# Router of a mixture-of-experts layer: which operand of the matmul is held in TensorE, the weights or the tokens

## The chip, the cores and the metric

One core of a Trainium2 chip runs the whole program: TensorE (matmul), VectorE, ScalarE, GpSimd, and SyncE, which issues most transfers. The metric is the device time of the kernel in microseconds; lower is better.

## The reference, cut to what matters

A two-layer decoder trunk over 512 prompt tokens and 8 sample tokens, with 1024 channels. Each layer has token mixers and then a feed-forward part: dense in layer 0, top-2 of 8 experts in layer 1.

```python
def moe_swiglu(h, w_router, b_router, w1, w3, w2):
    logits = h.astype(jnp.float32) @ w_router.astype(jnp.float32) + b_router.astype(jnp.float32)
    top_v, top_i = lax.top_k(logits, TOP_K)
    gates = jax.nn.softmax(top_v, axis=-1)
    comb = jnp.sum(jax.nn.one_hot(top_i, N_EXPERTS, dtype=jnp.float32) * gates[..., None], axis=-2)
    ...
    for e in range(N_EXPERTS):
        y = y + comb[..., e:e + 1] * swiglu(h, w1[e], w3[e], w2[e])
    return y
```

`h` has 520 rows of 1024 numbers, `w_router` is 1024 x 8, so the logits are 520 x 8.

## The kernel before, in words

Activations are held transposed: `hT` has the channels on the partitions, in 8 tiles `k` of 128 channels, and the 520 tokens along the free dimension (512 prompt tokens, then 8 sample tokens). The order of the work is written out by hand: each engine has its own program, in order, and semaphores tie them together. A matmul has a stationary operand, which is loaded into TensorE first, and a moving one, which streams past it; the output has the columns of the stationary operand on the partitions.

In the router (lines 943 to 950) the stationary operand is a tile of the router weights, `wrt[:, k, :]`, 128 x 8, and the moving one half of the tokens, 260 columns. The logits so come out with the 8 experts on the partitions, in two banks of `PP[0]`. The normalised and modulated `hT` for it is made just ahead: VectorE scales (line 1441), ScalarE adds the shift tile by tile (line 1197, semaphore `h`), and GpSimd does the 8 sample columns (lines 612 to 614, semaphore `hs`).

ScalarE adds the bias as it evicts the logits to `lgT` (line 1299; the bias is on 8 partitions, `brt[NE, 1]`). TensorE transposes `lgT` in five pieces (line 954), so that tokens are on the partitions, and VectorE copies the result from `PP[1]` to `lg` (lines 1627 and 1628). On `lg` VectorE finds the two largest logits of each token, their indices and a mask (to line 1643). Meanwhile TensorE transposes `hT` back to rows, 128 tokens at a time (`h_rows`, line 962), three tiles ahead of the mask and two behind it, in `PP[2]` and `PP[3]`; ScalarE copies them out (line 1303). Two matmuls on the mask (lines 969 and 970) count how many tokens stand ahead of each in its expert's list; from that VectorE works out each token's place (line 1662).

With the places, GpSimd scatters the rows to a table in DRAM sorted by expert (line 695, ten indirect transfers), SyncE gathers the first expert's rows (line 486), TensorE turns them (line 985), and the experts follow one after the other (lines 1014 and 1026). The code of an expert exists once for each width of its moving operand (144, 160, 176, 208, 256), and a branch on the token count chooses (line 1046).

The two loads of router weights and bias are issued by ScalarE at the very start (lines 1125 and 1126).

Of the kernel before, what the change touches and what calls it, by code (L numbers as in the profile page):

```python
# [9 lines left out]
ALU = mybir.AluOpType  # L10
ACT = mybir.ActivationFunctionType
AX = mybir.AxisListType

P = 128
D = 1024
KD = D // P
SEQ = 512
NS = 8
T = SEQ + NS
HT = T // 2  # L20
# [6 lines left out]
NE = 8  # L27
# [10 lines left out]
NT = (T + P - 1) // P  # L38
# [51 lines left out]
def trunk_program(nc, A, O):  # L90
    ctx = ExitStack()
    with ctx:
        def sb(name, shape, dt=F32):
            return ctx.enter_context(nc.sbuf_tensor(name, shape, dt))
# [19 lines left out]
        def sem(name):  # L114
            return ctx.enter_context(nc.semaphore(name))
# [4 lines left out]
        hT = sb_two("hT", [P, KD, T])  # L120
# [7 lines left out]
        ident = sb("ident", [P, P])  # L128
        ones = sb("ones", [P, P])
        eps = sb("eps", [P, 1])  # L130
        wrt = sb("wrt", [P, KD, NE])
        brt = sb("brt", [NE, 1])
        win = sb("win", [P, 2])
        winv = sb("winv", [P, 2])
        cinv = sb("cinv", [P, 2, POOL])
# [32 lines left out]
        stat2 = sb("stat2", [P, T])  # L168

        lg = sb("lg", [P, NT, NE])  # L170
# [4 lines left out]
        mask = sb("mask", [P, NT, NE])  # L175
# [8 lines left out]
        gate = sb("gate", [P, 2, NT])  # L184
# [33 lines left out]
        hflat = hT[:, :, :].rearrange("p k n -> p (k n)")  # L218
        gate_p, gate_s, gf, diag = (cut(hflat, i * D, D) for i in range(4))
        outs = work  # L220
        lgT = stat2[0:NE]

        def pair_raw(e, f):
            c, s0 = f // 3, (PER_E * e + 2 * (f // 3)) % EXPERT_RING
# [4 lines left out]
        PP = [ctx.enter_context(nc.psum_tensor(f"PP{q}", [P, 2, 512], F32)) for q in range(4)]  # L229
# [13 lines left out]
        def two(ap):  # L243

            return ap.rearrange("p (h n) -> p h n", h=2)
# [14 lines left out]
        wr_in = sem("wr_in")  # L260
# [30 lines left out]
        def norm_step(tag, k, n):  # L291
# [1 line left out]

        ff_done, ff_act, ff_free = sem("ff_done"), sem("ff_act"), sem("ff_free")
        fy_done, fy_free = sem("fy_done"), sem("fy_free")
        R = {k: sem(f"moe_{k}") for k in ["lg", "lg_ev", "lg_tr", "mask", "pre", "route", "gate",
                                          "zero", "h_tr", "h_row", "in_tr", "hn_odd", "hn_even", 
                                          "f_done", "f_act", "f_free", "y_done", "y_free", "yt_tr", "yt_ev",
                                          "y_out", "y_all", "count", "exp_d", "diag", "g_mm", "g_ev", "x_tr", "x_ev",
# [415 lines left out]
        def _(pe):  # L715
# [58 lines left out]
            for j in range(KD):  # L774
                tr = pe.transpose(PP[3][:, 0, j * NQ:(j + 1) * NQ], crow[0:NQ, j * P:(j + 1) * P], ident[0:NQ, 0:NQ])
# [7 lines left out]
            for l in range(DEPTH):  # L783
                with pe.Fori(0, NA) as i:
                    for j in range(ADA_RING):
                        n = 24 * l + ADA_RING * i + j
                        pe.wait_ge(ada_lo, n + 1)
                        pe.wait_ge(ada_row, n + 1)
                        for k in range(KD):
                            for lower, w in enumerate((ahi[:, j % 3], ada_slot(j))):  # L790
                                mm = pe.matmul(PP[0][0:2 * NQ, j % 2, 0:256], r_(cs[:, k, :]), r_(w[:, k, :]),  # L791
                                               start=(k == 0 and not lower), stop=(k == KD - 1 and bool(lower)))
                        mm.then_inc(ada_mm, 1)
                        if j % 3 == 2:
                            pe.wait_ge(ada_row, n + 3)
                            for m in range(2):
                                tr = pe.transpose(PP[1][:, 0, m * P:(m + 1) * P], modrow[:, m * P:(m + 1) * P], ident[:])
                            tr.then_inc(ada_tr, 1)
                if l == 0:
# [3 lines left out]
                    for v in range(DEPTH):  # L803
                        tr = pe.transpose(PP[3][:, 0, v * NROWS:(v + 1) * NROWS], rows[0:NROWS, v, :], ident[0:NROWS, 0:NROWS])
                    tr.then_inc(pro_tr, 1)
                    pe.wait_ge(x_in, 16 * NT)
                    for j in range(KD):
                        if j >= 2:
                            pe.wait_ge(*((pro_dve, 3 + j // 2) if j % 2 == 0 else (pro_act, j // 2)))
                        for t in range(4):  # L810
                            tr = pe.transpose(PP[2][:, j % 2, t * P:(t + 1) * P], xin[:, t, j * P:(j + 1) * P], ident[:])
                        tr.then_inc(pro_tr, 1)
                    for j in range(KD):
                        tr = pe.transpose(PP[3][:, 1, j * NS:(j + 1) * NS], xin[0:NS, 4, j * P:(j + 1) * P], ident[0:NS, 0:NS])
# [6 lines left out]
            for l in range(DEPTH):  # L821
# [7 lines left out]
                for h in range(4):  # L829
                    tr = pe.transpose(PP[3][:, 0, h * P:(h + 1) * P], ws_raw[:, h, :], ident[:])  # L830
                tr.then_inc(s["ws_tr"], 1)
                for ct in range(2):
# [5 lines left out]
                    tr = pe.transpose(PP[0][:, 0, 120 * ct:120 * ct + 120], stD[0:120, c], ident[0:120, 0:120])  # L838
# [28 lines left out]
                for n in range(4):  # L867
                    for ct in range(2):
                        tr = pe.transpose(PP[3][:, n // 2, (n % 2) * W + ct * P:(n % 2) * W + ct * P + P],
                                          proj[:, HOME[B_V] + ct, n * P:(n + 1) * P], ident[:])  # L870
# [5 lines left out]
                for n in range(4):  # L876
                    for ct in range(2):
                        mm = pe.matmul(PP[n // 2][:, n % 2, ct * 256:ct * 256 + 256], vtok[:, n, ct * P:(ct + 1) * P],
                                       wsT[:, 2 * ct:2 * ct + 2, :].rearrange("p h t -> p (h t)"), start=True, stop=True)
# [17 lines left out]
                for n, (a, m) in enumerate(zip(src, TAIL)):  # L897
                    for ct in range(2):
                        tr = pe.transpose(tail_bank(n)[0:m, ct * P:(ct + 1) * P], a[:, ct, :], ident[:])
# [18 lines left out]
                if l == 0:  # L918

                    for h in range(2):
                        if h:
                            pe.wait_ge(fy_free, KD)
                        for f in range(FH):
                            if f >= 2:
                                pe.wait_ge(ff_free, FH * h + f - 1)
                            if h == f == 0:
                                mm = two_products(0, U_FF(0, 0, 0), hT, hlo, range(KD), h_tile(1))
                            else:
                                for w in range(2):  # L930
                                    mm = product(2 * (f % 2) + w, U_FF(h, f, w), hT, hlo, range(KD))
# [12 lines left out]
            pe.wait_ge(*norm_step(3, "hs", 1))  # L944
            for k in range(KD):
                pe.wait_ge(*norm_step(3, "h", k + 1))
                for h in range(2):
                    gemm_r = pe.matmul(PP[0][0:NE, h, 0:HT], wrt[:, k, :], hT[:, k, HT * h:HT * h + HT],
                                       start=(k == 0), stop=(k == KD - 1))
            gemm_r.then_inc(R["lg"], 1)  # L950
            pe.wait_ge(R["lg_ev"], 1)
            for t in range(NT):
                n = min(P, T - P * t)
                tr = pe.transpose(PP[1][0:n, 0, t * NE:(t + 1) * NE], lgT[0:NE, P * t:P * t + n], ident[0:NE, 0:NE])
            tr.then_inc(R["lg_tr"], 1)

            def h_rows(t):
                n = min(P, T - P * t)
# [102 lines left out]
            with pe.If(counts[NE] > NW):  # L1061
                with pe.Fori(0, NE) as e:
                    for w in range(WINDOWS):
                        x = e * WINDOWS + (NE + w)
                        for t in range(2):
                            pe.wait_ge(Rin[t], reg(pe, 16 * x + 16))
                            for j in range(KD):
                                tr = pe.transpose(PP[t][:, j // 4, (j % 4) * P:(j % 4) * P + P], stage[:, t, j * P:(j + 1) * P], ident[:])
                            tr.then_inc(R["in_tr"], 1)
                        pe.wait_ge(R["hn_even"], reg(pe, 4 * x + (4 - 2 * NE)))  # L1070
                        for f in range(ET):
# [4 lines left out]
                            for v in range(2):  # L1076
                                for k in range(KD):
                                    mm = pe.matmul(PP[v][:, f % 2, 0:NW], raw[:, v, k, :], hn[:, k, :], start=(k == 0), stop=(k == KD - 1))
                            mm.then_inc(R["f_done"], 1)
                        pe.wait_ge(R["f_free"], reg(pe, ET * x + ET))  # L1080
                        for q in range(KD):
# [3 lines left out]
                            for k in range(ET):  # L1085
                                mm = pe.matmul(PP[2][:, q % 2, 0:NW], expert_slot(j, ET, 256)[:, k, P * (q % 2):P * (q % 2) + P],
                                               Gn[:, k, :], start=(k == 0), stop=(k == ET - 1))
                            mm.then_inc(R["y_done"], 1)
                        pe.wait_ge(R["y_free"], reg(pe, KD * x + KD))
                        for j in range(KD):  # L1090
                            if j % 4 == 0:
                                pe.wait_ge(R["yt_ev"], reg(pe, 4 * x + j // 2))
                            for t in range(2):
                                tr = pe.transpose(PP[3][:, t, (j % 4) * P:(j % 4) * P + P], yn[:, j, P * t:P * t + P], ident[:])
# [6 lines left out]
            for j in range(KD):  # L1101
                mm = pe.matmul(PP[0][:, j // 4, (j % 4) * P:(j % 4) * P + P], ones[:], diag[:, j * P:(j + 1) * P],
                               start=True, stop=True)
            mm.then_inc(R["g_mm"], 1)
            for j in range(KD):
                tr = pe.transpose(PP[1][0:NS, j // 4, (j % 4) * P:(j % 4) * P + P], mod[:, 1, 8 * GATE2 + j, 1:NQ], ident[:])
# [3 lines left out]
            for t in range(NT):  # L1110
                n = min(P, T - P * t)
# [10 lines left out]
        def _(act):  # L1122
            act.wait_ge(c_in, 32)
            act.activation(crow[0:NQ], crow[0:NQ], ACT.Silu).then_inc(silu_c, 1)
            act.dma_start(wrt[:], A["w_router"][0].rearrange("(k p) e -> p k e", p=P)).then_inc(wr_in, 16)
            act.dma_start(brt[:], A["b_router"][0].rearrange("(e a) -> e a", a=1)).then_inc(wr_in, 16)

            act.wait_ge(const_ready, 1)
            def root(q, dst, n, done):
# [73 lines left out]
            for l in range(DEPTH):  # L1203
# [70 lines left out]
                if l == 0:  # L1274
                    act.wait_ge(*step(l, "tail_out", 16 * 8))
                    for h in range(2):
# [3 lines left out]
                        for f in range(FH):  # L1280
                            n = FH * h + f
# [12 lines left out]
                                upper(U_FY(h, q) + UNIT_SLOTS)  # L1294

            act.wait_ge(R["lg"], 1)
            act.wait_ge(wr_in, 32)
            act.activation(two(lgT), PP[0][0:NE, :, 0:HT], ACT.Identity, bias=brt[:]).then_inc(R["lg_ev"], 1)
            for t in range(NT):  # L1300
                n = min(P, T - P * t)
                act.wait_ge(R["h_tr"], t + 1)
# [15 lines left out]
            for e in range(NE):  # L1318
                for f in range(ET):
                    n = ET * e + f  # L1320
# [48 lines left out]
        def _(dve):  # L1369
# [8 lines left out]
            def link(ins):  # L1378
                dve.wait_ge(dchain, done(ins))
# [243 lines left out]

            link(dve.memset(lg[:], 0.0))
            dve.wait_ge(R["lg_tr"], 1)
            dve.tensor_copy(lg[:, 0:4, :], PP[1][:, 0, 0:4 * NE].rearrange("p (t e) -> p t e", t=4))
            link(dve.tensor_copy(lg[0:NS, 4, :], PP[1][0:NS, 0, 4 * NE:5 * NE]))
            for t in range(NT):
                last = dve.max(vmax[:, t, :], lg[:, t, :])  # L1630
            link(last)
# [140 lines left out]
```

## Time and profile before

| | us |
|---|---|
| median of 3 runs | 1733.9 (1732.95 to 1734.55) |
| profiled execution | 1732.69 |
| its span | 1730.9 |
| TensorE matmul busy | 1488.1 (86%) |
| VectorE busy | 600.9 (35%) |
| ScalarE busy | 461.0 (27%) |
| GpSimd busy | 398.0 (23%) |

The span is the time from the first to the last instruction of one profiled execution. "PE" is TensorE's matmuls, "PEld" its loads of the stationary operand, which overlap them; "DVE" is VectorE, "ACT" ScalarE, "POOL" GpSimd, "SP" SyncE.
### The profile page before, as it was taken

How to read it: one execution, taken by the hardware profiler on the slowest of the kernel's cores; microseconds unless marked ns; L12 is line 12 of the kernel's file. 1: busy time of each engine (PE TensorE's matmuls, PEld its weight loads, DVE VectorE, ACT ScalarE, POOL GpSimd, SP SyncE). 2: the span in 40 equal slices, each digit the busy share in tenths (PEclk: the TensorE clock that was granted, in tenths of full speed). 3: DMA queues.
4: the chain of work that ended last, by engine and by line, in shares of the span. 5: the costliest groups of instructions: out<-in, count | busy, mean ns of one | idle time of the engine just before them, and what ended most of it. 6: DMA issues, size and time to landing. Idle time of an engine off the chain costs nothing.

```text
span 1730.9 us, 26002 instructions
## 1 busy us (share of the span) xinstructions
PE 1488.1 (86%) x11320; PEld 1425.0 (82%) x11320; DVE 600.9 (35%) x815; ACT 461.0 (27%) x646; POOL 398.0 (23%) x288
## 2 busy tenths in 40 slices
PE   5777794797999999998968784999999986999992
PEld 4555694697999999997957682999999986999992
DVE  6757598734102111014696622011110110010115
ACT  6767421433222122222313312111111110010114
POOL 1101571253344333443450512000000000000005
PEclk9999897899999999998988897999999997999995
DMA  9999231113423323233221027589789792658644
GB/s 319 326 308 348 67 98 32 41 59 118 126 74 100 108 74 98 58 101 98 74 73 49 6 71 271 193 272 334 242 286 318 271 309 76 216 164 300 228 146 169
DMA packets 249973, 286.70 MB, mean 166 GB/s; under 512 B 7469, under 2 KB 241599, under 8 KB 249814
## 3 DMA queue, kind: packets, MB, share of 16 engines
q1 hardware_dynamic: 244886, 272.17, 48.4%
q0 software_dynamic: 3760, 12.09, 1.9%
q8 instruction: 103, 1.69, 0.4%
q10 hardware_dynamic: 1200, 0.56, 0.1%
q14 instruction: 24, 0.20, 0.0%
HBM read 266.45 MB, written 19.07 MB: 165 GB/s over the span
## 4 chain that ended last, share of the span: by engine, by line
PE 71%; DVE 15%; DMA 5%; issue 4%; SPq 2%; ACT 2%; POOL 1%; POOLq 0%; DVEq 0%; ACTq 0%
PE PP L746 29%; PE PP L1014 21%; PE PP L1026 11%; DVE work L1499 7%; DMA mem<-in_w_ada 4%; PE PP L759 2%; PE PP L791 2%; DVE stat L1595 2%; PE PP L720 1%; PE PP L731 1%; PE PP L985 1%; PE PP L996 1%; DVE stat L1428 1%; DVE mem L1441 1%; DVE mem_r L1437 1%
## 5 line engine op out<-in xcount | busy, mean ns | idle before, releaser
L746 PE MATMUL PP<-hT_r,mem_r 128*128 128x260 f32 x2624 | 428.5, 284 | 4.6 <-DVE xT L1453 3.2
L1014 PE MATMUL PP<-big,mem 128*128 128x144 f32 (+2 forms) x2816 | 372.9, 295 | 22.8 <-issue 22.0
L1014 PEld LDWEIGHTS PP<-big,mem 128*128 128x128 f32 x2816 | 370.7, 191 | 23.5 <-issue 22.4
L604 POOL TENSOR_TENSOR mem_r<-mem,mem_r 128x1024 fp32r<-128x1024 f32 (+1 forms) x108 | 279.0, 2598 | 407.7 <-ACT mem_r L1141 407.0
L746 PEld LDWEIGHTS PP<-hT_r,mem_r 128*128 128x128 f32 x2624 | 362.5, 189 | 6.5 <-issue 2.5
L746 PE MATMUL PP<-mem_r 128*128 128x260 f32 x1312 | 263.8, 283 | 0.0
L746 PEld LDWEIGHTS PP<-mem_r 128*128 128x128 f32 x1312 | 201.7, 188 | 0.0
L1026 PE MATMUL PP<-big,mem 128*128 128x144 f32 (+2 forms) x1408 | 193.5, 294 | 0.0
L1026 PEld LDWEIGHTS PP<-big,mem 128*128 128x128 f32 x1408 | 186.6, 190 | 0.0
L1689 DVE TENSOR_TENSOR big<-PP,stat 128x256 f32<-128x256 f32 x88 | 37.4, 425 | 394.4 <-ACT stat L1324 394.4
L702 POOL DMA_INDIRECT mem<-y_by_expert,place x10 | 9.9, 986 | 624.5 <-SPq L534 621.8
L1141 ACT ACTIVATE mem_r<-mem 128x1024 fp32r<-128x1024 f32 (+1 forms) x108 | 115.9, 1099 | 118.5 <-DMA mem<-in_w_dense 70.9
L746 PE MATMUL PP<-big_r,mem_r 128*128 128x260 f32 x1056 | 129.4, 284 | 2.9 <-DVE big L1614 2.9
L746 PEld LDWEIGHTS PP<-big_r,mem_r 128*128 128x128 f32 x1056 | 127.7, 188 | 3.6 <-DVE big L1614 3.3
L1324 ACT ACTIVATE stat<-PP 128x256 f32<-128x256 f32 x88 | 33.8, 384 | 361.5 <-PE PP L1014 361.5
L1499 DVE SCALAR_TENSOR_TENSOR work<-big,vec,work 128x512 f32<-128x512 f32 x120 | 127.1, 1135 | 0.0
L1403 DVE TENSOR_TENSOR mem_r<-mem,mem_r 128x2048 fp32r<-128x2048 f32 x48 | 110.0, 2293 | 46.4 <-ACT mem_r L1157 46.4
L791 PE MATMUL PP<-mem_r,cs_r 128*18 128x256 f32 x768 | 104.0, 296 | 19.2 <-DVE mem_r L1403 18.4
L791 PEld LDWEIGHTS PP<-mem_r,cs_r 128*18 128x18 f32 x768 | 77.3, 103 | 43.2 <-DVE mem_r L1403 22.5
L1157 ACT ACTIVATE mem_r<-mem 128x2048 fp32r<-128x2048 f32 x48 | 91.7, 1911 | 25.1 <-DMA mem<-in_w_ada 25.1
L1614 DVE TENSOR_TENSOR big<-PP,work 128x520 f32<-128x520 f32 x22 | 15.4, 700 | 221.6 <-ACT work L1285 221.6
L759 PE MATMUL PP<-hT_r,mem_r 128*128 128x260 f32 x320 | 58.9, 304 | 28.4 <-POOL mem_r L618 25.9
(236 smaller groups left out, 1100.5 us busy)
## 6 DMA issues: line engine op xcount, KB each, us to landing
mem<-in_w_moe SPq DMA_DIRECT2D x48, 1536.0 KB, 8.8
mem<-in_w_ada SPq DMA_DIRECT2D x48, 1024.0 KB, 11.2
mem<-in_w_moe SPq DMA_DIRECT2D x32, 1408.0 KB, 9.4
mem<-in_w_dense SPq DMA_DIRECT2D x20, 1024.0 KB, 5.5
mem<-in_w_in SPq DMA_DIRECT2D x16, 1024.0 KB, 5.4
mem<-in_w_moe SPq DMA_DIRECT2D x16, 1024.0 KB, 6.8
mem<-in_w_dense SPq DMA_DIRECT2D x16, 704.0 KB, 4.7
mem<-in_w_out SPq DMA_DIRECT2D x8, 1024.0 KB, 5.1
```

Of the source, the lines that this page charges most:

```text
L604: pool.tensor_tensor(r_(raw), raw, read_(hi), ALU.subtract).then_inc(w_lo, 1)
L746: mm = pe.matmul(PP[q][:, h, 0:HT], r_(w[:, k, :]), r_(x[:, k, HT * h:HT * h + HT]), start=(i == 0 and w is wh and x is hi), stop=(i == le ...
L759: mm = pe.matmul(PP[q + c][:, h, 0:HT], r_(w[:, k, :]), r_(x[:, k, HT * h:HT * h + HT]), start=(i == 0 and w is wh and x is hi), stop=(i = ...
L791: mm = pe.matmul(PP[0][0:2 * NQ, j % 2, 0:256], r_(cs[:, k, :]), r_(w[:, k, :]), start=(k == 0 and not lower), stop=(k == KD - 1 and bool( ...
L1014: mm = pe.matmul(PP[w][:, f % 2, 0:n], raw[:, w, k, :], hn[:, k, 0:n], start=(k == 0), stop=(k == KD - 1))
L1026: mm = pe.matmul(PP[2][:, q % 2, 0:n], expert_slot(PER_E * e + 8 + q // 2, ET, 256)[:, k, P * (q % 2):P * (q % 2) + P], Gn[:, k, 0:n], sta ...
L1141: act.activation(r_(hi), raw, ACT.Copy).then_inc(w_hi, 1)
L1157: act.activation(r_(ahi[:, j % 3]), ada_slot(j), ACT.Copy).then_inc(ada_hi, 1)
L1403: dve.tensor_tensor(r_(ada_slot(j)), ada_slot(j), read_(ahi[:, j % 3]), ALU.subtract).then_inc(ada_lo, 1)
L1499: dve.scalar_tensor_tensor(acc, gin[:, ct, k:k + SEQ], tap("conv_c_w", k, ct), acc, ALU.mult, ALU.add).then_inc(s["conv_tap"], 1)
L1595: link(dve.reciprocal(st[:], st[:]))
L1689: dve.tensor_tensor(Gn[:, f, :], PP[1][:, f % 2, 0:NW], hactn[:, f % 2, :], ALU.mult).then_inc(R["f_free"], 1)
```

## The change

The operands of the router's matmuls trade places. For each channel tile `k`, four tiles of 128 tokens of `hT` become stationary, one after the other, and `wrt[:, k, :]` with its 8 columns moves past each. The four accumulate in four banks (`PP[0]` and `PP[1]`). The 8 sample tokens have a pass of their own behind that, with 8 stationary columns. The logits then have tokens on the partitions. ScalarE's eviction, the five transposes and the semaphores `lg_ev` and `lg_tr` go; VectorE reads the logits from PSUM and adds the bias itself, in five additions. The bias is loaded to all 128 partitions.

```diff
-        brt = sb("brt", [NE, 1])
+        brt = sb("brt", [P, NE])
...
-        lgT = stat2[0:NE]
...
             for k in range(KD):
                 pe.wait_ge(*norm_step(3, "h", k + 1))
-                for h in range(2):
-                    gemm_r = pe.matmul(PP[0][0:NE, h, 0:HT], wrt[:, k, :], hT[:, k, HT * h:HT * h + HT],
-                                       start=(k == 0), stop=(k == KD - 1))
-            gemm_r.then_inc(R["lg"], 1)
-            pe.wait_ge(R["lg_ev"], 1)
-            for t in range(NT):
-                n = min(P, T - P * t)
-                tr = pe.transpose(PP[1][0:n, 0, t * NE:(t + 1) * NE], lgT[0:NE, P * t:P * t + n], ident[0:NE, 0:NE])
-            tr.then_inc(R["lg_tr"], 1)
+                for t in range(4):
+                    mm = pe.matmul(PP[t // 2][:, t % 2, 0:NE], hT[:, k, P * t:P * t + P], wrt[:, k, :], start=(k == 0), stop=(k == KD - 1))
+            for k in range(KD):
+                mm = pe.matmul(PP[0][0:NS, 0, NE:2 * NE], hT[:, k, SEQ:T], wrt[:, k, :], start=(k == 0), stop=(k == KD - 1))
+            mm.then_inc(R["lg"], 1)
...
-            act.dma_start(brt[:], A["b_router"][0].rearrange("(e a) -> e a", a=1)).then_inc(wr_in, 16)
+            act.dma_start(brt[:], A["b_router"][0].rearrange("(a e) -> a e", a=1).to_broadcast([P, NE])).then_inc(wr_in, 16)
...
-            act.wait_ge(R["lg"], 1)
-            act.wait_ge(wr_in, 32)
-            act.activation(two(lgT), PP[0][0:NE, :, 0:HT], ACT.Identity, bias=brt[:]).then_inc(R["lg_ev"], 1)
...
             link(dve.memset(lg[:], 0.0))
-            dve.wait_ge(R["lg_tr"], 1)
-            dve.tensor_copy(lg[:, 0:4, :], PP[1][:, 0, 0:4 * NE].rearrange("p (t e) -> p t e", t=4))
-            link(dve.tensor_copy(lg[0:NS, 4, :], PP[1][0:NS, 0, 4 * NE:5 * NE]))
+            dve.wait_ge(wr_in, 32)
+            dve.wait_ge(R["lg"], 1)
+            for t in range(4):
+                dve.tensor_tensor(lg[:, t, :], PP[t // 2][:, t % 2, 0:NE], brt[:], ALU.add)
+            link(dve.tensor_tensor(lg[0:NS, 4, :], PP[0][0:NS, 0, NE:2 * NE], brt[0:NS], ALU.add))
```

## Rows read from the trace of the kernel before

**Rows 1.** The page: busy us (share of the span) x instructions, by engine.
```profile
PE 1488.1 (86%) x11320; PEld 1425.0 (82%) x11320; DVE 600.9 (35%) x815; ACT 461.0 (27%) x646; POOL 398.0 (23%) x288
```

**Rows 2.** Chain in order of time, 1028 to 1082: start us, us, what.
```profile
1037.75 9.78 PE PP L948 x32
...
1047.56 0.69 ACT stat L1299
...
1048.30 0.45 PE PP L954 x5
...
1052.72 0.21 DVE mask L1643
...
1057.65 0.18 DVE place L1662
```

**Rows 3.** Stretches: busy us (x count) by engine, then PEclk, DMA share, GB/s.
```profile
1037.70:1043.00 5.30, 5.25 (x13) 1.67 (x14) 3.87 (x7) 4.57 (x7) 0.00 (x0) 0.50 1.06 372
1043.00:1047.60 4.60, 4.52 (x21) 1.66 (x19) 0.00 (x0) 0.04 (x1) 0.00 (x0) 1.00 1.06 373
```

**Rows 4.** Timeline, router: start us, us, engine line op out<-in xcount [idle before].
```profile
1037.75 9.77 PE L948 MATMUL PP<-hT,wrt 128*8 128x260 f32 x32 [6.09 <-POOL hT L614]
...
1042.04 0.13 PEld L948 LDWEIGHTS PP<-hT,wrt 128*8 128x8 f32 x1 [0.30 <-issue]
...
1043.19 3.82 PEld L948 LDWEIGHTS PP<-hT,wrt 128*8 128x8 f32 x18
```

**Rows 5.** Timeline of the mask matmuls; line 1102: min/median/max ns, starts.
```profile
1052.97 0.30 PEld L969 LDWEIGHTS PP<-mask,tri 128*128 128x128 f32 x2 [1.24 <-DVE mask L1643]
1053.19 0.30 PEld L970 LDWEIGHTS PP<-mask,ones 128*128 128x128 f32 x2
...
L1102 PEld LDWEIGHTS PP<-hT,ones x16: 287/333/333, 1692.3 to 1695.5; 128*128 128x128 f32 x16
```

**Rows 6.** Transposes that move 8 columns: timeline; min/median/max ns, starts.
```profile
92.28 0.66 PE L814 MATMUL PP<-ident,big 8*128 8x8 f32 x8
...
L814 PE MATMUL PP<-ident,big x8: 200/201/223, 92.3 to 92.7; 8*128 8x8 f32 x8
```

**Rows 7.** Timeline of VectorE, the two copies of the logits.
```profile
1048.85 0.19 DVE L1627 COPY lg<-PP 128x32 f32<-128x32 f32 x1 [7.28 <-PE PP L954]
1048.95 0.14 DVE L1628 COPY lg<-PP 8x8 f32<-8x8 f32 x1
```

**Rows 8.** Timeline, TensorE's transposes of the first three row tiles.
```profile
1048.66 1.97 PE L962 MATMUL PP<-ident,hT 128*128 128x128 f32 x16
...
1050.87 1.09 PE L962 MATMUL PP<-ident,hT 128*128 128x128 f32 x8 [0.24 <-ACT work L1303]
```

**Rows 9.** Stretches in the prologue, each with the one that follows it.
```profile
90.75:94.10 3.35, 1.84 (x18) 1.42 (x16) 1.37 (x3) 1.94 (x4) 0.00 (x0) 1.00 0.60 176
94.15:97.50 3.35, 3.35 (x8) 2.67 (x9) 0.00 (x0) 3.35 (x7) 0.00 (x0) 0.50 0.99 337
29.30:32.60 3.30, 1.64 (x13) 1.01 (x12) 3.10 (x2) 2.44 (x3) 0.00 (x0) 1.00 1.10 352
32.70:36.00 3.30, 3.24 (x28) 2.42 (x26) 0.93 (x2) 2.17 (x2) 1.18 (x4) 1.00 1.10 349
```

**Rows 10.** Stretches behind the start of two bursts.
```profile
1442.30:1445.70 3.40, 3.40 (x10) 3.31 (x11) 0.00 (x0) 0.00 (x0) 0.00 (x0) 0.50 0.02 5
1445.85:1449.00 3.15, 3.15 (x20) 3.15 (x19) 0.00 (x0) 0.00 (x0) 0.00 (x0) 1.00 0.00 0
...
1695.00:1698.30 3.30, 3.30 (x18) 2.64 (x17) 1.68 (x2) 1.15 (x1) 2.39 (x4) 0.50 0.88 322
```

**Rows 11.** Chain at a branch between experts; the page's queue of instructions.
```profile
1422.66 19.54 issue
...
q8 instruction: 103, 1.69, 0.4%
```

**Rows 12.** Transfers of the first 40 us: the queue of the router's weights.
```profile
q10 hardware_dynamic: 1056, 0.03, 2.2%
```

More of the change, by code:

```diff
@@ L295, in trunk_program @@
         fy_done, fy_free = sem("fy_done"), sem("fy_free")
-        R = {k: sem(f"moe_{k}") for k in ["lg", "lg_ev", "lg_tr", "mask", "pre", "route", "gate",
+        R = {k: sem(f"moe_{k}") for k in ["lg", "mask", "pre", "route", "gate",
                                           "zero", "h_tr", "h_row", "in_tr", "hn_odd", "hn_even",
```

## The prediction, before the result was known

> **What bounds the kernel now.** I read the page first: TensorE is busy for 86% of the span and no other engine for more than 35% [rows 1]. The profiled execution took 1732.69 us, of which 1730.9 are the span; the median of the three timed runs is 1733.9, so 1.2 us are added at the end to whatever the sum gives on this profile. Then I read the chain in order of time around the router [rows 2]. The reader is to see that every step there hangs on the one before: 16 router matmuls (32 instructions, since each float32 matmul is issued twice) from 1037.75 to 1047.53, ScalarE's eviction at 1047.56, five transposes at 1048.30, VectorE's top-2 work up to the mask at 1052.72+0.21, the places at 1057.65, and behind them ten scatters by GpSimd, the gather, and the experts, for which TensorE has to wait. So nothing absorbs a shift of the mask: what the router gains or loses reaches the end of the kernel one to one, unless the clock adds something of its own.
>
> Third, the granted clock by stretch [rows 3]. TensorE had been idle for 6 us [rows 4]; the router starts at the lower of the two levels, 1.2 GHz (0.50 in the row), and runs 5.3 us there before the rest goes at 2.4 GHz. Per instruction that is 0.13+0.30 = 0.43 us from load to load at half clock and 3.82/17.5 = 0.22 us from load to load at full [rows 4]; 12.2 instructions at the first and 19.8 at the second make 5.28+4.3 = 9.6 us, which is the 9.78 of the chain.
>
> **The change, part by part.**
>
> *Router matmuls.* The stationary operand grows from 8 columns to 128 (a token tile of hT), the moving one shrinks from 260 to 8. There are 8 x 4 = 32 matmuls of this kind, 64 instructions, and 8 more for the sample tokens (stationary 8 columns, moving 8), 16 instructions. An instruction that moves only 8 columns is bound by its load. What a float32 load of 128 columns costs in the two-pass form is shown by the two mask matmuls, which move 40 columns: their first loads start 0.22 us apart with two in each, so 0.11 us each at full clock [rows 5]. At half clock the nearest is the gate broadcast, line 1102, 16 instructions with loads of 128 and moves of 128: (1695.5-1692.3)/15 = 0.213 us each, at 0.50 [rows 5, 10]. It moves as many columns as it loads, so 0.213 is an upper bound for the load alone, and 0.11 (no slower than at full clock) the lower. I take 0.213: a load there lasts 333 ns against 0.30-0.11 = 0.19 us for the same form in the mask matmuls, and everything else on TensorE doubles too.
>
> The Trainium skill, "TensorE: Matmul & The Clock Gate", section "LDWEIGHTS (loading the stationary operand)", gives a load's time as its columns over 1.2 and nothing for the clock level: 107 ns for 128 columns. At full clock the mask rows agree (0.11). By it the 64 would take 6.8 us at either level; the 333 ns loads speak against that at the lower one.
>
> *Sample matmuls.* Nearest are the small transposes, 8 columns moved: (0.66-0.20)/7 = 0.066 us each [rows 6]. At half clock between 0.066 and 0.13; I take 0.07, since such short ones look bound by issue. 16 x 0.07 = 1.1 us.
>
> *The clock.* This decides. Does the new stream, which moves 8 columns per load, bring the clock up at 1043 as the old one did, which moved 260? At half clock the whole router takes 64 x 0.213 = 13.6, plus 1.1, plus 0.2 for the last to come out: done at 1052.7. If it rises at 1043.03 after 5.28 us: 24.8 instructions at 0.213, 39.2 at 0.11 (4.3 us), then 1.1+0.2: done at 1048.6. No stretch of the trace has such a stream alone, so both stand. The nearest is 90.75 to 94.10: TensorE is busy 1.84 us, with the eight small transposes (8 columns moved, 128 loaded) among its 18, and the clock is at half right behind it; 29.30 to 32.60, busy only 1.64 us but with moves of 256 and 128 columns, stays at full [rows 6, 9]. Short moves did not hold the clock where shorter busy time with long moves did. I read this as: the clock stays at half through the new router.
>
> *Eviction and transposes gone.* ScalarE's step and the five transposes end at 1048.75; VectorE starts at 1048.85 [rows 2, 7]. All 1.2 us behind 1047.53 go. ScalarE has nothing else to do then, so only the path counts.
>
> *VectorE.* Two copies become five additions that read PSUM. Before: the second starts 0.10 after the first and lasts 0.14, so 0.24. After: 4 x 0.10 + 0.14 = 0.54. Plus 0.3 on the path [rows 7]. The two waits in front are on the router and on a DMA of the first 40 us; queued behind them are only VectorE's own top-2 steps.
>
> *TensorE behind the router.* The three row tiles of transposes that come ahead of the mask matmuls take 1.97 us for two tiles at full clock, and the third waits for ScalarE's copy of the first [rows 8]. Before, they ended at 1051.96, 1 us ahead of the mask. At half clock the first sixteen take 16 x 0.213 = 3.4 (1052.6 to 1056.0) and the third tile is done by 1057.2 if the clock rises meanwhile, 1057.9 if not. VectorE has the mask at 1052.93+4.2 = 1057.1. So this is about hidden, and costs up to 1 us if the clock stays low through the mask matmuls.
>
> *Loads at the start.* The bias goes to 128 partitions instead of 8: 120 more tiny packets beside 1056 of that queue that take 2.2% of 16 engines over 40 us [rows 12], by share 120/1056 x 0.022 x 40 = 0.1 us. The transfers there are on the path; I add 0.1.
>
> **Sum.** Clock low: VectorE starts at 1052.7+0.1 = 1052.8 against 1048.85, so +3.95; +0.3 for the additions; +0.1 at the start: +4.35, or 1737.0 for the profiled execution and, by the median, 1738.3. Its bounds: sample matmuls at 0.13 (+0.9), the transposes not hidden (+1), and the old router's time at half clock: the burst that begins at 1442.2 is at half for 3.6 us, the one at 1692.3 for 6.0 [rows 5, 10], so in other executions the old one may take up to 0.9 us less, and the loss is that much larger. Below, 0.5 from sizes. That is 1737.5 to 1740.5, with the lower bound of the load (0.11, 7 us for the 64) left to the rival below.
>
> **Rivals.**
> 1. *The clock rises as before.* VectorE at 1048.7, -0.15, +0.3, +0.1: +0.25, so 1734.2. For it: loads keep TensorE busy without a gap, and by busy time alone it is as full as before. Against it: the stretch at 90.75. By the Trainium skill, same page, section "What's actually happening", the gate follows how busy TensorE has been and the number of matmuls does not matter; by that rule this rival would come true.
> 2. *Loads cost what they do in the small transposes* (other side, not slower). These load 128 columns too and come every 0.066 us. If the router's did so, at half clock 0.13: 64 x 0.13 = 8.3, +1.1+0.2, done at 1047.4: VectorE at 1047.5, -1.35+0.3+0.1 = -0.95; with the clock rising at 1043, 40 at 0.13 and 24 at 0.066: done at 1045.9, -2.5. It decides once the load is under 0.145 us at half clock (9.3 us for the 64, which leaves the mask where it was). 1731.4 to 1733. Against it: the mask matmuls, of the very form, at 0.11 at full clock.
> 3. *Code loading at a branch.* TensorE waits 19.5 us at 1422.66 for nothing the profile shows, and instructions come in 103 packets [rows 11]. The change adds 86 TensorE instructions (160 for 74) ahead, which at 1.69 MB for 26002 instructions (65 bytes each) move what follows by 5.6 KB, a third of a packet. A jump that needs one fetch more or less, a quarter of 19.5, is 5 us either way: 1733.4 or 1743.2. For it: the gap is large; against it: the jumps go far, and most will miss as before.
>
> **How the numbers follow.** Clock low: 0.76. Rival 1: 0.13. Rival 2: 0.03. Rival 3: 0.08, half each way. A measurement of this kernel can tell about 0.2%, 3.5 us. The low clock gives slower nearly always (0.69 of its 0.76), with rival 3's upper half 0.73; same takes rival 1, 2 and the small end of the first, 0.25; faster 0.02. The predicted time is the likeliest's, 1738.3. The range reaches down to rival 1 (1734.2) and up to 1740.5.
>
> **What would show it.** The granted clock from 1043 to 1052: 0.50 if I am right, 1.00 if rival 1 is. The loads of 128 columns in the router: 0.213 us apart at half clock, 0.11 at full, 0.13 or 0.066 for rival 2. From the router's end to VectorE's first addition 0.1 us; from there to the mask 0.3 us more than now. ScalarE idle until the first row copy. The transposes of the row tiles begin at half clock. The wait at 1422 keeps its 19.5 us unless rival 3 holds. I am wrong if the mask is ready within 1 us of 1052.9, or if the mask moves by 4 us and the end does not.

## The result, and the profile after

The changed kernel takes 1752.3 us (median of six runs, 1747.6 to 1756.3); the kernel before, on the same chip, 1734.3 us (six runs, 1733.0 to 1735.0). The ratio is 1.0106, with a 95% interval of 1.0088 to 1.0123: 15 to 21 us slower. The prediction was 1738.3 with a range of 1734.2 to 1740.5. Its sign is right; the time lies 12 us above its upper end.

The profiled execution of the changed kernel took 1747.59 us, the lowest of its six, against 1732.69 before; the spans differ by 13.8 us. So the traces account for some 14 us, and what the other executions add on top isn't in them.

Lines of the page of the changed kernel: its span, the busy times and two DMA queues. They answer to [rows 1] and to the queue of instructions in [rows 11]; the queue q10, which carries the router's weights and bias, had 1200 packets over the whole of the kernel before:

```profile
span 1744.7 us, 26089 instructions
PE 1497.9 (86%) x11363; PEld 1440.4 (83%) x11363; DVE 599.4 (34%) x818; ACT 460.5 (26%) x645; POOL 398.3 (23%) x288
q8 instruction: 105, 1.72, 0.4%
q10 hardware_dynamic: 1328, 0.56, 0.1%
```

TensorE has 43 more matmul records with a load each, the 86 instructions of the prediction. It is busy for 9.8 us more [rows 1]. ScalarE has one instruction fewer, VectorE three more: as intended.

**The router.** The chain of waits of the changed kernel around it, in order of time, which answers to [rows 2]:

```profile
1037.35 13.79 PE PP L947 x64
1051.14 0.49 PE PP L949 x16
1051.63 5.00 PE PP L957 x24
...
1061.04 0.18 DVE place L1656
```

The 64 router instructions take 13.8 us, where 32 took 9.78. The eviction and the five transposes are gone. But behind them three row tiles of transposes (line 957) now stand on the chain, where before VectorE's mask stood. The places, the last thing the router hands on, start 23.69 us behind the router's start, against 1057.65 - 1037.75 = 19.90 before [rows 2]: the router costs 3.8 us by this measure.

What the router loses shows in the granted clock of these stretches of the changed kernel (the columns are those of [rows 3]):

```profile
1037.50:1046.00 8.50, 8.50 (x41) 8.50 (x41) 3.66 (x7) 4.37 (x7) 0.00 (x0) 0.50 1.06 373
1046.00:1055.50 9.50, 9.50 (x60) 9.44 (x60) 3.62 (x31) 1.25 (x2) 0.00 (x0) 0.50 1.03 363
```

TensorE is busy without a gap in both and yet stays at 0.50 (1.2 GHz) for the whole router, where the old one had 1.00 (2.4 GHz) from 1043 on [rows 3]. Its loads are at the slow rate, as their line shows (min/median/max ns, first and last start):

```profile
L947 PEld LDWEIGHTS PP<-wrt,hT x64: 288/333/333, 1037.3 to 1050.7; 128*128 128x128 f32 x64
```

(1050.7 - 1037.3)/63 = 0.213 us from one load to the next.

**Behind the router.** The rest of the loss sits 100 to 600 us later, in code that the change does not touch. The chain of waits of the changed kernel, at the starts of the experts' code (144 columns wide, but 208 for expert 5 and 160 for expert 6; "issue" is time in which TensorE waited for nothing that the profile shows):

```profile
1084.66 43.36 PE PP L1009 x352
...
1152.87 2.43 issue
1155.30 9.68 PE PP L1009 x64
...
1225.33 1.90 issue
1227.23 3.67 PE PP L1009 x28
1230.90 1.99 issue
...
1300.24 1.46 PE PP L1009 x10
1301.71 1.53 issue
...
1438.56 15.16 issue
1453.72 14.06 PE PP L1009 x64
...
1552.88 2.51 issue
1555.38 4.45 PE PP L1009 x31
1559.84 1.06 issue
```

The same chain of the kernel before had one long stall at 1422.66 [rows 11] and one short one, ahead of expert 6:

```profile
1149.89 7.84 PE PP L1014 x64
...
1540.56 2.43 issue
1542.99 8.93 PE PP L1014 x64
```

Expert 1 used to start without a gap and now waits 2.43 us; experts 2, 3 and 6 stop a second time inside their first matmuls. Nine waits (with 0.66 us ahead of expert 3 and 0.41 us ahead of expert 7, which the lines leave out) add up to 27.7 us, where two made 22.0: 5.7 us more. And behind a stall the first 64 matmuls are slower: 9.68 us instead of 7.84 for expert 1. The clock in these stretches of the changed kernel goes with it; the kernel before had 1.00 at the same place (1149.90 to 1157.70):

```profile
1155.35:1158.20 2.85, 2.85 (x12) 2.85 (x13) 0.00 (x0) 0.00 (x0) 0.00 (x0) 0.50 1.06 397
1158.20:1165.00 6.80, 6.80 (x56) 6.80 (x55) 0.42 (x1) 0.39 (x1) 0.00 (x0) 0.97 0.08 24
```

Summed over the seven later experts (1.84, 2.18, 0.40, 0, 0.79, 0.27, 0.24) the slow starts cost 5.7 us. With the 3.0 us by which the first expert matmul is later (1084.66 against 1081.68) that makes 14.4 us, for 13.8 us of span.

What an expert waits for can be read from the DMA view of short stretches, in the queue that carries instructions (packets, MB, share of the 16 engines). First two stretches inside the 15.16 us of the changed kernel, 1443.9 to 1444.9 and 1448.7 to 1449.7, then one just ahead of expert 1's wait, 1151.8 to 1152.8:

```profile
q8 instruction: 2, 0.03, 23.9%
q8 instruction: 2, 0.03, 24.5%
q8 instruction: 1, 0.02, 5.8%
```

In the long wait packets of instructions move in pairs, some 5 us from one pair to the next, and nothing between. The changed kernel has two pairs in its 15.16 us, the kernel before three in its 19.54 us (at 1427.5, 1432.3 and 1437.5). So it is the round that has a price, some 5 us each: one round fewer is 4.4 us less. In none of the changed kernel's short waits does a packet move. There TensorE goes on 2.5 to 3.2 us behind the last single packet (1152.4 and 1155.30 for expert 1, 1230.2 and 1232.89 for the second stop of expert 2), and some 4.5 us behind a pair. That fits code which can be used only some time after its packet shows in the profile; the profile doesn't say which instructions a packet held.

### The profile page after: what moved, and what is told of

Read it like the earlier page. It is cut to its first block, busy times and chain, and to the rows that moved or that the text cites. A ratio compares the mean times of both kernels' runs of the same rounds, so it can differ in the third digit from the quotient of the medians.

```text
span 1744.7 us, 26089 instructions
## 1 busy us (share of the span) xinstructions
PE 1497.9 (86%) x11363; PEld 1440.4 (83%) x11363; DVE 599.4 (34%) x818; ACT 460.5 (26%) x645; POOL 398.3 (23%) x288
## 3 DMA queue, kind: packets, MB, share of 16 engines
q10 hardware_dynamic: 1328, 0.56, 0.1%
## 4 chain that ended last, share of the span: by engine, by line
PE 71%; DVE 15%; DMA 5%; issue 4%; SPq 2%; ACT 2%; POOL 1%; POOLq 0%; DVEq 0%; ACTq 0%
PE PP L745 29%; PE PP L1009 22%; PE PP L1021 11%; DVE work L1491 7%; DMA mem<-in_w_ada 5%; PE PP L758 2%; DVE stat L1587 2%; PE PP L790 1%; PE PP L719 1%; PE PP L730 1%; PE PP L980 1%; SPq L432 1%; PE PP L991 1%; PE PP L947 1%; DVE stat L1420 1%
## 5 line engine op out<-in xcount | busy, mean ns | idle before, releaser
L1009 PE MATMUL PP<-big,mem 128*128 128x144 f32 (+2 forms) x2816 | 378.0, 297 | 28.5 <-issue 27.7
```

Source lines behind the costliest of these rows:

```text
L1009: mm = pe.matmul(PP[w][:, f % 2, 0:n], raw[:, w, k, :], hn[:, k, 0:n], start=(k == 0), stop=(k == KD - 1))
```

## The experiments

Each was timed against the kernel before on the same chip. The first four ran on one chip, the last four on another; the kernel before took 1733.6 us on both (median of 21 runs each).

**1. The kernel before, with 86 idle-time instructions.** Nothing of the change is in it; only what follows is moved by as many TensorE instructions as the change moves it. The 43 small transposes run while TensorE waits for the places, and their results are not used.

```diff
             for t in range(3, NT):
                 h_rows(t)
+            for _ in range(43):
+                pe.transpose(PP[1][0:NE, 1, 0:NE], ident[0:NE, 0:NE], ident[0:NE, 0:NE])
             pe.wait_ge(R["route"], 1)
```

> The kernel before, its router untouched, with 43 transposes of 8x8 into unused columns of PP[1], put where TensorE has nothing to do (behind the last row tile of h, ahead of the wait for the places). They are 86 TensorE instructions, so the experts' code stands exactly as far back as in the changed kernel. They take about 43 x 0.066 = 2.8 us in a wait of 20 us.
> Theory A (placement of the code): the changed router costs 3.5 to 4.5 us by its own work, and the remaining 13 to 14 us of the 18 are instruction packets that come late because the experts' code is shifted against the packets. This kernel then takes 1744 to 1752 us, with stalls for no reason the profile shows at the start of experts 1 to 3.
> Theory B (the new router itself, or the later time at which the experts start, brings the stalls): 1734 to 1736 us, and only the old two stalls (19.5 and 2.4 us).

Measured: 1747.6 us (1743.9 to 1751.5), ratio 1.0082 (1.0064 to 1.0100). Its chain of waits:

```profile
1149.95 2.09 issue
...
1222.14 1.85 issue
1223.99 3.67 PE PP L1016 x28
1227.66 2.31 issue
...
1297.03 1.46 PE PP L1016 x10
...
1435.02 15.43 issue
...
1552.59 4.45 PE PP L1016 x31
```

The stalls come at the same places of the code as in the changed kernel, behind 28, 10 and 31 matmuls, and the long one takes 15.43 us with, again, four packets. So the shift of the code by itself costs 14 us (11 to 17), with the old router untouched. The work of the 43 transposes is no rival: they take 1.2 us in idle time, and experiment 2 runs 85 of them without a loss. It also has the wider spread of the changed kernel (7.5 us over four runs).

**2. The changed kernel, shifted to a total of 256 instructions** (85 of the same small transposes, 170 instructions, in the same place). 1.69 MB in 103 packets [rows 11] are 16.4 KB each, and at 65 bytes an instruction about 250. By the Trainium skill, "Advanced Engine Details and Errata", section "ISA Cache", a line holds 16KB, which is 256 instructions. With 256 more ahead, all that follows should lie in its packets as it did before the change.

> The changed kernel with 85 such transposes (170 instructions) in the same place: with the router's own 86 the shift is 256 instructions. An instruction packet of 16 KB holds 256 instructions of 64 bytes, so the experts' code stands against the packets as it did before the change. They take 5.6 us in a wait of 20.
> Theory A: the stalls of experts 1 to 3 go, the wait at expert 5 is back at 19 to 20 us, and the time is 1737.5 to 1740 (1734.3 plus what the router itself costs).
> Theory B: 1750 to 1755, as the changed kernel.

Measured: 1736.9 us (1735.3 to 1739.6), ratio 1.0017 (1.0008 to 1.0026). Its chain of waits has the two stalls of before and no other:

```profile
1038.80 13.79 PE PP L947 x64
...
1427.49 19.28 issue
...
1545.37 2.74 issue
```

The Trainium skill's 256 agrees with that, though no neighbouring total was tried. With the placement of before, the change costs 3.2 us (1.4 to 4.5), and the other 15 us of its loss are gone. Experiments 1 and 2 come at the code shift from both sides: 13.9 us when it is added alone, 14.8 when it is taken away alone (18.0 less 3.2, each against its own runs of the kernel before).

**3. As 2, but each router matmul moves 128 columns instead of 8:** the same weights, sixteen times over, of which VectorE reads the first eight. Loads, instructions and their number are unchanged.

```diff
-                    mm = pe.matmul(PP[t // 2][:, t % 2, 0:NE], hT[:, k, P * t:P * t + P], wrt[:, k, :], ...)
+                    mm = pe.matmul(PP[t // 2][:, t % 2, 0:16 * NE], hT[:, k, P * t:P * t + P],
+                                   wrt[:, k:k + 1, :].to_broadcast([P, 16, NE]), ...)
```

> As the one before, but each of the 64 long router instructions moves its 8 columns sixteen times over (128 columns, the same 8 of the router's weights repeated); the count of instructions and of loads is the same, and the logits are read from the first eight columns.
> Theory C (what keeps the clock low in the new router is that only 8 columns move per load): the granted clock rises about 5 us into the router as in the kernel before, the remaining instructions come every 0.11 instead of 0.213 us, and the router ends 3.5 to 4 us earlier than with 8 columns; 1734 to 1736 us.
> Rival D (the stream of loads of 128 columns itself keeps the clock low, or costs more than 128 moved columns can hide): the clock stays at 0.50, the router takes 13.8 us or more, the time is that of the run before or above.

Measured: 1733.6 us (1732.2 to 1735.4), ratio 0.9998 (0.9989 to 1.0007). The chain of waits at the router, and then two stretches of it by the clock:

```profile
1039.14 9.93 PE PP L947 x64
```
```profile
1037.80:1043.00 5.20, 3.86 (x18) 3.89 (x19) 5.15 (x9) 4.81 (x8) 1.16 (x2) 0.50 1.06 373
1043.60:1048.50 4.90, 4.90 (x42) 4.90 (x42) 0.00 (x0) 0.06 (x1) 0.00 (x0) 0.91 1.06 372
```

Sixteen times the work per matmul makes the router 3.9 us shorter, since the clock now rises within it: a mean of 0.91 over the second stretch is 0.9 us at half and 4.0 at full clock, so it rose at 1044.5, 5.3 us into the router. The kernel is 3.3 us faster than 2 and even with before (1.9 us less to 1.2 more). So within what these runs can tell the low clock is the whole cost of the changed router, and it comes from how little each instruction moves.

**4. The kernel before, with the branches that choose an expert's width put together.** Before, the test for the next width lies behind the code of the last one, so that a jump to the widest code goes from one to the next; now all tests of an expert come first, then its five versions of the code.

```diff
-                pe.br_lt(c, n + 1, on_true=here, on_false=f"expert{e}_over_{n}")
-                with nc.body(here, valid_engines=[pe.engine]):
-                    expert(e, n, c)
-                with nc.body(f"expert{e}_over_{n}", valid_engines=[pe.engine]):
-                    by_width(e, c, widths[1:])
+                for i, n in enumerate(widths[:-1]):
+                    ...  pe.br_lt(c, n + 1, on_true=to[i], on_false=test[i + 1])
+                for i, n in enumerate(widths):
+                    with nc.body(to[i], valid_engines=[pe.engine]):
+                        expert(e, n, c)
```

> The kernel before with the branches that choose an expert's width put together: the four tests stand one behind the other ahead of the first body, where each test used to stand behind the body of the width before it. One unconditional branch per expert is added; the bodies are the same.
> Theory E (the 19.5 us wait ahead of expert 5 is three jumps in a row into code that isn't there, each to fetch before the next test can be read, and then the body): with the tests together only one jump is left to fetch. The wait falls to 3 to 6 us, the kernel to 1718 to 1722 us, if the shift by 4 to 11 instructions brings no new stall.
> Rival F (the wait is not the tests but the start of the 208 wide body, or a semaphore): it stays at 15 to 20 us, the kernel at 1733 to 1736.

Measured: 1726.2 us (1725.8 to 1728.9), ratio 0.9955 (0.9939 to 0.9972). Its chain of waits:

```profile
1355.19 2.22 issue
1357.41 9.75 PE PP L1014 x64
...
1427.52 7.93 issue
```

The long stall shrinks from 19.5 to 7.9 us, with two instruction packets in it instead of six. The tests' place is what made it long; that each fetch began only when the one before had brought the next test fits the packets, and is argued from them. Both expectations were missed, 3 to 6 us for the wait and 1718 to 1722 us for the time: two packets are left, and not one, at 1431.0 and 1432.4, and the edit moved the code too: expert 4 now has a stall of 2.22 us with a slow start behind it (9.75 for 7.84). 11.6 us won less 2.2 and 1.9 given back are 7.5, which is the difference of the medians. The spans differ by 6.4 only, since the router of this profiled execution starts 1.05 us later (1038.80), with no edit ahead of it.

**5. The kernel before, with the clock brought up ahead of the router.** Thirteen matmuls of 128x260, whose results are not used, run in the 6 us in which TensorE waits for hT; 102 small transposes bring the shift back to that of before in packets.

```diff
             pe.wait_ge(wr_in, 32)
+            for _ in range(13):
+                pe.matmul(PP[3][:, 1, 0:HT], ones[:], xT[:, 0, 0:HT], start=True, stop=True)
             pe.wait_ge(*norm_step(3, "hs", 1))
```

> The kernel before with 13 matmuls (128 stationary, 260 moving columns, 26 instructions, result not used) in the 6 us that TensorE is idle ahead of the router, and 102 small transposes in the idle time behind the row tiles of h, so that the experts' code is shifted by exactly 256 instructions.
> Theory C (the clock is low at the router's start because TensorE idled ahead of it, and wide moves keep it up): the router runs at 1.00 throughout, 32 x 0.22 = 7.0 us instead of 9.8; 2 to 3 us less than before, 1731 to 1732 us. No new stall at an expert.
> Rival G (the 13 matmuls delay the router or slow the engines that write hT): 1733 to 1736 us.

Measured: 1730.2 us (1728.5 to 1732.9), ratio 0.9980 (0.9971 to 0.9989): 3.4 us faster. The old router takes 7.19 us instead of 9.78, at full clock from end to end:

```profile
1040.50:1047.60 7.10, 7.09 (x32) 2.80 (x32) 3.86 (x7) 4.57 (x7) 0.00 (x0) 1.00 1.06 373
```

**6. The changed kernel with the same thirteen matmuls** (and 59 small transposes behind). It asks whether the new stream can at least hold a clock that is up when it starts.

> The changed kernel with the same 13 matmuls ahead of the router, and 59 small transposes behind, shift 256 in all; it is to be compared with the one that has the 170 padding instructions alone (1736.9).
> Theory C: the router with 8 moved columns starts at full clock and loses it on the way, since its own stream does not hold it: a first part of 3.5 to 7 us at 0.11 per instruction, the rest at 0.213. 1732.5 to 1735 us.
> Theory H (once up, any gapless stream of loads holds the clock; the low clock of the changed kernel is only that of its start): 1.00 throughout, the router takes 64 x 0.11 = 7.0 us, 1729.5 to 1731 us.

Measured: 1737.5 us (1732.6 to 1740.4), ratio 1.0015 (1.0004 to 1.0025). By the clock of its router:

```profile
1038.00:1040.20 2.20, 1.84 (x18) 1.82 (x17) 2.20 (x5) 2.20 (x4) 0.32 (x1) 1.00 1.07 376
1040.20:1050.50 10.30, 10.30 (x52) 10.28 (x52) 2.03 (x4) 2.74 (x5) 0.00 (x0) 0.50 1.06 374
```

It can't: 1.8 us into the router the clock falls and stays down, with TensorE busy without a gap. The router is 1.6 us shorter than in 2 (12.15 us), and the places come 21.76 us behind its start instead of 24.02. Yet the time isn't lower than that of 2, and it lies above the 1732.5 to 1735 that was expected. In the profiled execution what was won is given back at the experts. The first of them starts at half clock here and not in 2. First the stretch of this kernel, then that of experiment 2:

```profile
1084.10:1088.00 3.90, 3.90 (x16) 3.90 (x17) 0.00 (x0) 1.06 (x1) 0.00 (x0) 0.50 0.00 0
```
```profile
1086.55:1090.50 3.95, 3.95 (x32) 3.95 (x33) 0.00 (x0) 1.06 (x1) 0.00 (x0) 1.00 0.00 0
```

Sixteen instructions where 2 has 32 in the same time: 1.9 us. Another 1.7 us goes at expert 6, whose first 64 take 10.61 us behind a wait of 2.72, and 8.93 behind one of 2.74 in 2. The level an expert finds after 20 us of small work and idling differs from kernel to kernel, and, as the spread of 7.8 us suggests, perhaps from run to run; the latter is not shown.

**7. and 8. The gains put together.** Experiment 7 is the kernel before with the edits of 4 and 5 (and 96 small transposes); experiment 8 is the changed kernel with those of 3, 4 and 5 (and 53).

> The kernel before with the matmuls ahead of the router, with the branches of an expert's width put together, and with 192 padding instructions, which put the end of each expert 8 to 12 instructions earlier in its packet than the version with the branches together had it. There a stall of 2.2 us had come ahead of expert 4, whose predecessor ended 6 instructions into a new packet; now it ends 6 before one.
> Theory A: that stall is gone (2 to 3 us less with its time at low clock); with theory C's 2 to 3 us: 1720 to 1722.5 us.
> Rival: the gains don't add, because another place now falls on the edge of a packet: 1723 to 1727 us.

> As the run before, with the changed router in its wide form (8 columns moved sixteen times over) in place of the old one, 106 padding instructions, the same placement of the experts' code.
> Theory C: at full clock from the start the 64 long instructions take 7.0 us and the 16 short 0.5, no eviction and no transposes: 0.3 to 1 us less than with the old router (7.0+1.2), 1719.5 to 1722 us.
> Rival: the tiles of hT come every 0.68 us and the wide form asks 0.88 for each, so both are paced alike, and the five additions eat the rest: equal within 0.3 us.

Measured: 7 takes 1720.6 us (1718.5 to 1722.8), ratio 0.9925 (0.9911 to 0.9938); 8 takes 1719.9 us (1719.0 to 1720.7), ratio 0.9920 (0.9907 to 0.9934). The chain of 7, then that of 8:

```profile
1038.20 7.19 PE PP L950 x32
...
1419.97 10.14 issue
```
```profile
1039.16 7.41 PE PP L949 x64
...
1421.01 9.62 issue
```

The clock of 8 over its router:

```profile
1039.16:1046.57 7.41, 7.41 (x67) 7.29 (x68) 3.86 (x7) 4.57 (x7) 0.00 (x0) 1.00 1.07 374
```

The stall of 4 ahead of expert 4 is gone in both. Both beat the kernel before and the changed one, 7 by 0.7% and 8 by 0.8% on the kernel before. Between them, 0.7 us is no difference that these runs can tell: the changed router is now as good as the old one (7.41 + 0.50 us without an eviction, against 7.19 and an eviction with transposes), and no better.

## Why the prediction was wrong in size and right in sign

**What failed: the step from the mask to the end, where the sum puts the moved code at nothing, and the price of rival 3.** The runs showed some 14 us in its place (13.9 in experiment 1, 14.8 between the changed kernel and experiment 2). The prediction said that "what the router gains or loses reaches the end of the kernel one to one". It reached it (+3.0 us at the first expert matmul), and then the experts lost 11 us more by themselves. The mechanism was written down as rival 3, with the right count of instructions (86, a third of a packet), at a chance of 0.08 and "5 us either way". Both numbers were wrong, for three reasons:

- I priced only the one long gap at 1422.66, by a quarter more or less. The shift hits the starts of six of the seven later experts, all but expert 4's: it made seven new waits of 0.4 to 2.4 us in the changed kernel, at places where the trace of before shows nothing at all. The long one became shorter, by 4.4 us, near the 4.9 I had for it, so by itself it helped.
- A stall also lets the clock fall. The slow start behind a gap was among my rows, 3.6 us at half clock from 1442.2 [rows 10], but I used it for the old router's spread only. It doubled the price: 5.7 us of waits, 5.7 us of slow starts.
- The chance. "Most will miss as before" was right for the long jump and not for the short ones. With seven later experts, each with code to be fetched at its start, a change of the pattern was the likelier case, as I see it now; of the kernels timed, three (the changed one, experiments 1 and 4) had new stalls and the others none.

"The wait at 1422 keeps its 19.5 us unless rival 3 holds": it went to 15.16. That the sign came out right is in part luck: the router's own 3.2 us has it, but 15 of the 18 us come from the code's place, for which the prediction left the sign open. The range has a slip of its own: its terms give 1737.8 to 1741.1, not 1737.5 to 1740.5, which doesn't matter at 1752.

**The clock: right.** 0.50 from 1037.4 to beyond 1055, as forecast. Experiment 3 shows the reason too: same loads, more columns, and the clock rises. Rival 1 is refuted by the changed kernel's own trace, and again by 2 and 6. Its rule, from the Trainium skill's "TensorE: Matmul & The Clock Gate", section "What's actually happening", that the gate follows how busy TensorE is and that the number of matmuls doesn't matter, does not describe this stream: it is gapless in the profile and stays at half.

**The load: right.** 0.213 us from load to load at half clock, the value taken, on average over the 64. The load time without a clock level that the same page of the Trainium skill gives (section "LDWEIGHTS (loading the stationary operand)") does not hold at half clock: the 64 took 13.8 us, not the 6.8 that it gives; at full clock (7.41 us for 64 in experiment 8, 0.116 each) it is near. Rival 2 needed 0.145 or less and is refuted.

**The small terms.** The sample matmuls: 16 in 0.49 us, 0.03 each at half clock, where the prediction had 0.07 and 1.1 us; 0.6 too much. VectorE's additions and the mask, from the changed kernel's timeline of VectorE:

```profile
1051.77 0.38 DVE L1621 TENSOR_TENSOR lg<-PP,brt 128x8 f32<-128x8 f32 x4 [10.61 <-PE PP L949]
...
1055.83 0.20 DVE L1637 TENSOR_TENSOR mask<-pick 128x40 f32<-128x40 f32 x1
```

The four additions take 0.38 us, with the fifth 0.44 (0.54 predicted, 0.24 for the copies before). The first comes 14.4 us behind the router's start, where the prediction had 15.05. The mask is ready at 1056.03, but the 24 row-tile transposes at half clock end at 1056.63 (1051.63 and 5.00 in the chain). These are the "up to 1 us if the clock stays low", and it was 0.6: what the sample matmuls gave, the lost cover took. So the places are 3.8 us later by the router's own start, for a predicted 4.25 (3.95 and 0.3). The bias brought 128 more tiny packets (1328 for 1200), not 120, and what they cost can't be told: the router starts 0.4 us earlier than before, and over the six profiled executions with nothing new ahead of the router but the bias it starts anywhere from 1037.35 to 1039.14. By the router's own start the first expert matmul is so 3.4 us later, and not 3.0.

Without the shift, the router's price in time is that of experiment 2: 3.2 us for 4.35 predicted. That would have been 1737 against the 1738.3 of the forecast, and inside its range.

**What stays open.** Why a given expert start stalls and another does not. The stalls inside an expert (behind 28, 10 and 31 matmuls) are the same in two kernels with the same shift, and fit a packet that came too late; but no rule for the stalls at the jumps, some of which have a branch hint (line 1034 of the kernel before), was found that explains all of them. And the changed kernel's median is 4.7 us above its profiled execution, with a spread of 8.7 us; experiment 1 has a like one, experiments 2 and 3 have 4.3 and 3.2. That late packets vary from run to run would explain it, and has not been shown; experiment 6, with the placement of before and no new stall, spreads by 7.8 us over eleven runs, so placement can't be all of it.

## What to carry to other kernels

In a long unrolled program the code itself is data that arrives late: count the instructions that an edit adds or removes on the engine that sets the end, ahead of its jumps, and before blaming or crediting the edit time a copy in which idle-time instructions restore the old placement. Where TensorE has an "issue" wait at the start of a block, suspect a fetch, move the code to see whether it goes, and count the slow clock behind it; tests that lie behind long bodies belong together (7.5 us here). Where TensorE's instructions load much and move little, look at the granted clock before counting them: a router with 8 moving columns ran at half clock with no gap in it, and the same loads with 128 moved columns were faster.

## What the runs showed that was not expected

- A gapless stream of 128-column loads with 8 moved columns neither brings the clock up (0.50 over 13.8 us) nor holds it: in experiment 6 it fell 1.8 us into the stream. With 128 moved columns it rose after 5.3 us in experiment 3, and in experiment 8 it stayed at 1.00 for all 7.4 us.
- Instructions shifted by 86 places cost 14 us without any work in them; shifted by 256, nothing of it. The short waits for code took 0.4 to 2.7 us each. The long one goes by rounds of some 5 us, with a pair of packets between one and the next: 19.54 us with three pairs, 15.16 with two, 10.14 with one. Only in experiment 4 did its two packets come 1.4 us apart, and it took 7.93.
- Float32 matmul instructions with 8 stationary and 8 moved columns come every 0.03 us even at half clock (16 in 0.49). The transposes of [rows 6], which move 8 columns too but load 128, came every 0.066 us at full clock, and so were a poor measure for them; the 43 transposes of experiment 1, which load 8, took 1.22 us at full clock, 0.03 us each.
